# Seven block products in place of eight for the branch gates, and another order of the input projection, in a two-layer diffusion backbone

## What is computed

```python
h = rms_norm(x, p['norm1_w']) * (1 + sc1) + sh1
proj = h @ p['w_in']
hy, qkv, scv, gates = jnp.split(proj, [HY_COLS, HY_COLS + ATT_COLS, HY_COLS + ATT_COLS + SC_COLS], axis=-1)
...
ya = hyena_mixer(hy, ...)
q, k, v = jnp.split(qkv, [ATT_Q, ATT_Q + ATT_KV], axis=-1)
...
ga, gb, gc = jnp.split(gates, 3, axis=-1)
merged = (jax.nn.sigmoid(ga) * (ya @ p['w_br_a'])
          + jax.nn.sigmoid(gb) * (yb @ p['w_br_b'])
          + jax.nn.sigmoid(gc) * (yc @ p['w_br_c']))
```

## Time and profile before

| | us |
|---|---|
| median of 3 runs | 2319.89 (2317.75 to 2322.31) |
| the profiled execution (span from its first instruction to its last) | 2318.0 |
| TensorE busy in it (matmuls) | 2186.4 |
| VectorE, ScalarE, GpSimd busy | 1435.7, 1006.0, 184.3 |
| mean granted TensorE clock | 0.972 of full speed |

### The profile page before, as it was taken

One profiled execution on the slowest core, in us unless ns is written; L12 is line 12 of the kernel. 1 busy time (PEld: TensorE's weight loads), 2 busy tenths in 40 slices (PEclk: granted clock), 3 DMA queues, 4 the chain that ended last, 5 costly groups with the idle time before them and its releaser, 6 DMA issues.

```text
span 2318.0 us, 35033 instructions
## 1 busy us (share of the span) xinstructions
PE 2186.4 (94%) x13382; PEld 1763.0 (76%) x13382; DVE 1435.7 (62%) x2009; ACT 1006.0 (43%) x1486; POOL 184.3 (8%) x224
## 2 busy tenths in 40 slices
PE   7998999999988998799997999999998999699999
PEld 2447999999656997466666999999864899366665
DVE  4865532612677555899996443431368763699997
ACT  2433212223622124688884321222461222588885
POOL 0010000010100100121110000001100110011210
PEclk8999999999998999899998999999999999799999
DMA  9772222333313522999993122132413342699997
GB/s 355 262 265 97 73 73 74 112 122 113 140 48 125 174 86 91 383 388 379 387 393 112 57 81 80 70 135 104 159 59 126 134 144 73 243 386 386 387 378 273
DMA packets 72954, 436.14 MB, mean 188 GB/s; under 512 B 9289, under 2 KB 9929, under 8 KB 31930
## 3 DMA queue, kind: packets, MB, share of 16 engines
q1 hardware_dynamic: 46368, 331.89, 37.4%
q0 software_dynamic: 22160, 88.61, 11.8%
q10 hardware_dynamic: 4300, 13.90, 1.8%
HBM read 384.87 MB, written 49.50 MB: 187 GB/s over the span
## 4 chain that ended last, share of the span: by engine, by line
PE 77%; DVE 9%; ACT 4%; DMA 3%; issue 3%; DVEq 2%; ACTq 0%; POOL 0%; POOLq 0%
PE ps L637 39%; PE ps L1119 9%; PE ps L1145 5%; PE ps L1123 4%; PE ps L839 4%; PE ps L1149 2%; PE ps L736 2%; PE ps L718 2%; PE ps L896 2%; DVE back L1933 1%; PE ps L676 1%; DMA front<-kspec 1%; DVE nb L1902 1%; ACT front_r L1213 1%; ACT front L1406 1%
## 5 line engine op out<-in xcount | busy, mean ns | idle before, releaser
L637 PE MATMUL ps<-front_r 128*128 128x320 f32 x5696 | 899.6, 311 | 14.2 <-DVE back_r L1993 8.2
L637 PEld LDWEIGHTS ps<-front_r 128*128 128x128 f32 x5696 | 854.0, 189 | 16.6 <-DVE front_r L1604 8.9
L1604 DVE TENSOR_TENSOR front_r<-ring,front_r 128x1024 fp32r<-128x1024 f32 x148 | 181.1, 1224 | 467.6 <-ACT front_r L1213 466.5
L1213 ACT ACTIVATE front_r<-ring 128x1024 fp32r<-128x1024 f32 x180 | 190.0, 1056 | 376.8 <-PE ps L637 291.7
L1213 ACT ACTIVATE back<-ps 128x256 f32<-128x256 f32 (+4 forms) x176 | 88.5, 518 | 376.7 <-PE ps L637 152.6
L2087 DVE TENSOR_TENSOR back_r<-front,back_r 128x1024 fp32r<-128x1024 f32 x128 | 153.3, 1219 | 4.9 <-ACT back_r L1213 3.2
L1119 PE MATMUL ps<-back_r 128*80 128x512 f32 x384 | 152.1, 396 | 3.7 <-ACT back_r L1213 3.7
L1119 PE MATMUL ps<-back_r,front_r 128*80 128x512 f32 x384 | 151.9, 396 | 0.0
L637 PE MATMUL ps<-back_r,front_r 128*128 128x320 f32 x640 | 148.1, 313 | 0.0
L1213 ACT ACTIVATE back_r<-front 128x1024 fp32r<-128x1024 f32 x128 | 133.4, 1054 | 7.7 <-PE ps L1149 4.9
L1372 ACT ACTIVATE back<-ps 128x640 f32<-128x640 f32 x48 | 33.8, 704 | 227.2 <-PE ps L637 227.1
(11 more groups left out here) (250 smaller groups left out, 3200.6 us busy)
## 6 DMA issues: line engine op xcount, KB each, us to landing
ring<-in_stream SPq DMA_DIRECT2D x186, 1024.0 KB, 7.3
front<-in_stream SPq DMA_DIRECT2D x80, 1024.0 KB, 18.2
back<-in_stream SPq DMA_DIRECT2D x48, 1024.0 KB, 19.2
gates<-back POOLq DMA_DIRECT2D x48, 320.0 KB, 2.4
back<-gates POOLq DMA_DIRECT2D x48, 320.0 KB, 3.3
kspec<-back POOLq DMA_DIRECT2D x20, 512.0 KB, 7.1
front<-kspec POOLq DMA_DIRECT2D x4, 2048.0 KB, 11.0
rows<-front ACTq DMA_DIRECT2D x10, 520.0 KB, 3.9
```

The lines of the kernel that those rows point to most:

```text
L637: mm = pe.matmul(tokh(b)[:, c0:c1], w(wp)[:, k, :], src(hp, k)[:, c0:c1], start=first, stop=last)
L1213: return act.activation(o, i, ACT.Copy)
L1604: dve.tensor_tensor(half_dst(u, 1), src, half_dst(u, 0).bitcast(F32), ALU.subtract).then_inc(w_lo, 1)
```

## The change

A gate item keeps its 256 columns, but is laid out as four blocks of 512 inputs x 128 columns (weights A11, A12, A21, A22), and the tokens as four blocks too (inputs 0 to 511 or 512 to 1023, tokens 0 to 319 or 320 to 639). The four output blocks are made of seven block products in place of eight (Strassen's scheme in Winograd's form). A product (`product`) is 4 x 3 = 12 matmuls of 320 columns, so a group of seven is 84 where two chunks were 96. Two products are accumulated on others in PSUM; the other sums are made elsewhere:

- Four sums of weight blocks for each group, by GpSimd (`pool.tensor_tensor` on 128 x 512), into `wsum`.
- Four sums of token blocks for each layer, by VectorE (`token_sum`), split into parts by ScalarE (`sum_hi`) and VectorE (`sum_lo`).
- Seven operands of 128 x 512 for each group in place of two halves of 128 x 1024: high part on ScalarE (`operand_hi`), low part on VectorE (`operand_lo`), in four places `WG`.
- Five additions of a product in PSUM to a partial result in SBUF for each group, on VectorE (`gate_sum`); a copy and two sigmoids on ScalarE (`gate_taken`).

The layer's order becomes: queries, keys and values (now tile by tile behind the norm, `first_qkv`), gates, hyena, short convolution. The transposes of queries and keys stand behind chunks 9 to 14 of the hyena and short convolution, the prompt's scores behind chunk 16. The preparation of queries and keys on VectorE is cut into 19 pieces (`prepare`), behind products 0 and 2 of each group. The stores of gates move from GpSimd's queue to SyncE's, one of 640 KB behind the load of an item. The prompt's filter spectrum (`Kp`) is loaded behind the attention's end, with a semaphore of its own.

```diff
-P_HY = 0
+P_QKV = 0
+P_GATE = P_QKV + N_QKV
+P_HY = P_GATE + N_GATE
 P_SC = P_HY + N_HY
-P_QKV = P_SC + N_SC
-P_GATE = P_QKV + N_QKV
-P_BR = P_GATE + N_GATE
+P_BR = P_SC + N_SC
 P_WO = P_BR + N_BR
...
+        WG = region_r(40, [4, 2, 512])
+        T_hi, T_lo, T_x = region_r(56, [4, 4, TH]), region_r(76, [4, 4, TH]), region(76, [4, 4, TH])
+        sgb, wsum = region(121, [2, 4, TH]), region(131, [4, 512])
...
+        qT, kT = region(66, [4, T]), region(137, [P + PAST + LS])
...
+        SUMS = {1: 1, 3: 2, 4: 0, 6: 3}
+        BLOCKS = {0: 0, 2: 1, 5: 3}
+        def operand(l, n):
+            g, j = n // 7, n % 7
+            if j in SUMS:
+                return wsum[:, SUMS[j], :]
+            return home(place(l, P_GATE + g))[:, 512 * BLOCKS[j]:512 * BLOCKS[j] + 512]
+        def block_of(l, g, b):
+            return home(place(l, P_GATE + g))[:, 512 * b:512 * b + 512]
+        def wait_operand_place(eng, l, n):
+            wait_half_used(eng, l, U_GATE + n - 4 if n >= 4 else U_GATE - 2 + n // 2)
...
+                    i = g - place(l, P_GATE) - 4
+                    if 0 <= i < N_GATE:
+                        sp.wait_ge(sg_ready, l * N_GATE + i + 1)
+                        sp.dma_start(a["gates"][2 * i:2 * i + 2].rearrange("i p n -> p i n"),
+                                     sgb[:, i % 2].rearrange("p (i h) n -> p i (h n)", i=2)).then_inc(sg_stored[i % 2], 16)
...
+                pool.wait_ge(t_raw, 4 * (l + 1))
+                apart(pool)
+                for g in range(N_GATE):
+                    u = l * UNITS + U_GATE + 7 * g
+                    at = place(l, P_GATE + g)
+                    a11, a12, a21, a22 = (block_of(l, g, b) for b in range(4))
+                    pool.wait_ge(landed[slot_of(at)], landing(at))
+                    if g:
+                        pool.wait_ge(w_lo, u - 2)
+                    apart(pool)
+                    pool.tensor_tensor(wsum[:, 0, :], a21, a22, ALU.add).then_inc(w_sum, 1)
+                    pool.wait_ge(w_sum, l * 4 * N_GATE + 4 * g + 1)
+                    apart(pool)
+                    pool.tensor_tensor(wsum[:, 1, :], wsum[:, 0, :], a11, ALU.subtract).then_inc(w_sum, 1)
+                    pool.tensor_tensor(wsum[:, 2, :], a11, a21, ALU.subtract).then_inc(w_sum, 1)
+                    if g:
+                        pool.wait_ge(w_lo, u)
+                    pool.wait_ge(w_sum, l * 4 * N_GATE + 4 * g + 2)
+                    apart(pool)
+                    pool.tensor_tensor(wsum[:, 3, :], a12, wsum[:, 1, :], ALU.subtract).then_inc(w_sum, 1)
...
+                def first_qkv():
+                    for k in range(KC):
+                        if k % 4 == 0:
+                            half_ready(l, k // 4)
+                        pe.wait_ge(x_lo, l * OP + k + 1)
+                        for t in range(NT):
+                            for wp, hp in ((0, 0), (0, 1), (1, 0)):
+                                mm = pe.matmul(ps[:, t + 2 * (t // 4), 0:256], h_part(hp, k)[:, P * t:P * t + P],
+                                               w2(k // 4, 4, wp)[:, k % 4, :], start=k + wp + hp == 0,
+                                               stop=k == KC - 1 and wp == 1)
+                            if k == 3 and t == NT - 1 or k == KC - 1 and t in (1, 3, 4):
+                                mm.then_inc(qkv_ready, 1)
+                first_qkv()
+                for i in range(1, N_QKV):
+                    qkv_item(i)
...
+                def tokens_of(j, part):
+                    if j in (0, 2, 6):
+                        r0, c0 = ((0, 0), None, (4, 0), None, None, None, (4, TH))[j]
+                        return lambda k: (h_hi, h_lo)[part][:, r0 + k, c0:c0 + TH]
+                    t = {4: 0, 1: 1, 3: 2, 5: 3}[j]
+                    return lambda k: (T_hi, T_lo)[part][:, t, k, :]
+                def product(n):
+                    g, j = n // 7, n % 7
+                    bank = (0, 1, 0, 2, 4, 3, 4)[j]
+                    pe.wait_ge(w_lo, l * UNITS + U_GATE + n + 1)
+                    if j == 6:
+                        pe.sem_inc(item_used, 1)
+                    if g == 0 and j in (0, 1, 3, 5):
+                        pe.wait_ge(qkv_freed, 9 * l + (7 if j < 2 else 8))
+                    if g and j in (0, 1, 3, 5):
+                        pe.wait_ge(gate_act, (l * N_GATE + g) * 3 - 1)
+                        pe.wait_ge(gate_dve, (l * N_GATE + g) * 5 - (3 if j else 4))
+                    if j == 2:
+                        pe.wait_ge(gate_act, (l * N_GATE + g) * 3 + 1)
+                    if g and j in (3, 4, 5):
+                        pe.wait_ge(gate_dve, (l * N_GATE + g) * 5)
+                    if j == 6:
+                        pe.wait_ge(gate_dve, (l * N_GATE + g) * 5 + 3)
+                    hi, lo = tokens_of(j, 0), tokens_of(j, 1)
+                    w = WG[:, n % 4].rearrange("p a (k m) -> p a k m", k=4)
+                    for k in range(4):
+                        for wp, x in ((0, hi), (0, lo), (1, hi)):
+                            mm = pe.matmul(ps[:, bank, 0:TH], w[:, wp, k, :], x(k),
+                                           start=k == 0 and wp == 0 and x is hi and j not in (2, 6),
+                                           stop=k == 3 and wp == 1, skip_group_check=j in (2, 6))
+                    mm.then_inc(gate_made, 1)
+                pe.wait_ge(x_lo, l * OP + OP_Y)
+                for n in range(PRODUCTS):
+                    product(n)
...
+                for c in range(24):
+                    half_ready(l, U_HY + c)
+                    if c == 0:
+                        pe.wait_ge(gate_act, (l + 1) * 3 * N_GATE - 1)
+                        pe.wait_ge(gate_dve, (l + 1) * 5 * N_GATE - 4)
+                    elif c < 3:
+                        pe.wait_ge(gate_dve, (l + 1) * 5 * N_GATE - 2 + c)
+                    else:
+                        wait_chunk_freed(pe, l, c - 3)
+                    chunk(c % 3, lambda part: w2(c, KC, part), h_part, KC).then_inc(chunk_ready, 1)
+                    if 1 <= c <= 8:
+                        transposes(c - 1)
+                    if c == 9:
+                        pe.wait_ge(tr_evac, l * 8 + 8)
+                        pe.wait_ge(prep_done, l + 1)
+                        apart(pe)
+                    if 9 <= c <= 9 + NT:
+                        turn_qk(c - 9)
+                    if c == 16:
+                        prompt_scores()
...
+                        wait_chunk_freed(pe, l, 21)
+                        wait_chunk_freed(pe, l, 22)
+                        wait_chunk_freed(pe, l, 23)
...
+                def operand_hi(n):
+                    g, j = n // 7, n % 7
+                    wait_operand_place(act, l, n)
+                    if j in SUMS:
+                        act.wait_ge(w_sum, (l * N_GATE + g) * 4 + SUMS[j] + 1)
+                    elif j == 0:
+                        at = place(l, P_GATE + g)
+                        act.wait_ge(landed[slot_of(at)], landing(at))
+                    copy(WG[:, n % 4, 0, :], operand(l, n)).then_inc(w_hi, 1)
+                def gate_taken(n):
+                    g, j = n // 7, n % 7
+                    out, G = sgb[:, g % 2], l * N_GATE + g
+                    if j == 0:
+                        act.wait_ge(gate_made, l * PRODUCTS + n + 1)
+                        if G >= 2:
+                            act.wait_ge(sg_stored[g % 2], 16 * (G // 2))
+                        copy(out[:, 0, :], ps[:, 0, 0:TH]).then_inc(gate_act, 1)
+                    elif j == 2:
+                        act.wait_ge(gate_made, l * PRODUCTS + n + 1)
+                        act.wait_ge(gate_dve, 5 * G + 1)
+                        act.activation(out[:, 0, :], ps[:, 0, 0:TH], ACT.Sigmoid).then_inc(gate_act, 1)
+                    elif j == 6:
+                        act.wait_ge(gate_dve, 5 * G + 5)
+                        act.activation(out[:, 1:4, :], out[:, 1:4, :], ACT.Sigmoid).then_inc(gate_act, 1)
+                        act.drain().then_inc(sg_ready, 1)
...
+                for n in range(4):
+                    operand_hi(n)
+                for n in range(PRODUCTS):
+                    gate_taken(n)
+                    if n + 4 < PRODUCTS:
+                        operand_hi(n + 4)
+                    if n == 17:
+                        act.wait_ge(qs_ready, l + 1)
+                        act.activation(st5[:], st5[:], ACT.Sqrt, bias=eps[:, 0:1], scale=1.0 / HD).then_inc(qrt, 1)
+                    if n >= PRODUCTS - 2:
+                        split_after(l, U_HY + n - PRODUCTS + 2, U_HY - 3 + 2 * (n - PRODUCTS + 2))
...
+                def operand_lo(n):
+                    dve.wait_ge(w_hi, l * UNITS + U_GATE + n + 1)
+                    dve.tensor_tensor(WG[:, n % 4, 1, :], operand(l, n), WG[:, n % 4, 0, :].bitcast(F32),
+                                      ALU.subtract).then_inc(w_lo, 1)
+                def gate_sum(n):
+                    g, j = n // 7, n % 7
```

(39 more changed lines are left out.)

407 lines of the change are left out of this document (193 added, 214 removed).

## The result

| | before | changed |
|---|---|---|
| median of the runs, us | 2318.82 | 2360.69 |
| lowest to highest, us | 2314.52 to 2322.31 | 2358.47 to 2366.5 |
| ratio to before | | 1.0191, interval 1.0171 to 1.021 |
| span of the profiled execution, us | 2318.0 | 2357.0 |

What follows compares the result with a forecast made beforehand. TensorE's work was taken as the bound; -21.2 - 3.95 + 0.4 + 0.8 + 5.6 = -18.3 us a layer, -36.7 for two, gave 2281.3 against the profiled 2318.0, so 2283 for the median, range 2270 to 2355.

Steps and rivals of the forecast that it cites:

- What bounds the kernel: Stage between norm and attention: TensorE's work is the bound, its neighbours have room, so fewer matmuls are time won.
- Term 1: Gate products: 144 fewer matmuls of 320 columns at 0.147 us, -21.2 us for a layer.
- Term 2: TensorE's waits around transposes, gates and hyena go, -3.95 us; a longer wait before the scores adds 0.4.
- Term 3: Layer's start, from norm to first gate product: waits for ScalarE and reordered work cost +0.8 us a layer.
- the edge that it named: Layer's start: VectorE ready at about +19.4, just in time for the third item of queries, keys and values.
- Term 5: GpSimd's four weight sums a group, about 1.2 us each, hidden under TensorE; cost to VectorE taken as nothing.
- Term 4: Rhythm of a gate group: product 6 waits up to 0.8 us for VectorE's sum 4, +5.6 us a layer.
- the rule of the lock: VectorE with two SBUF inputs and a GpSimd instruction reading SBUF exclude each other for a whole instruction.
- The rival: Gate groups: GpSimd's sums shut out VectorE's two-input instructions for their whole length; about 2351 us, chance 0.32.

Runs made afterwards that it cites:

- e4: The changed kernel with VectorE's preparation pieces left out, only their signals kept (output not the reference's): 2280.23 us.
- e10: e6 with ScalarE's first copies ahead of the first token sum, the 960-element sigmoid later, and GpSimd's sums starting only after the token operands: 2274.96 us.
- e7: The changed kernel with the weight sums made by VectorE and the preparation pieces spread, one a group behind product 0: 2311.14 us.
- e1: The changed kernel with GpSimd's weight sums replaced by signals, except in layer 0's first group (output not the reference's): 2294.54 us.
- e8: e7 with ScalarE's first copies of queries, keys and values put ahead of the first token sum: 2306.78 us.
- e9: e8 with ScalarE's 960-element sigmoid moved behind the next group's first copy and rounding: 2275.16 us.
- e6: The changed kernel, sums still on GpSimd, with preparation pieces spread: one a group behind sum 5, two in groups 9 and 10, four in the hyena part: 2325.12 us.
- e5: The changed kernel with the weight sums made by VectorE in place of GpSimd, pieces where they were: 2327.8 us.

## Why the prediction was wrong, step by step

**What bounds the kernel.** Right that TensorE does. "Its neighbours have room" held for their sum, not for VectorE's stretch from product 0 to sum 4.

**Term 1** was right: in e4 the gates of layer 0 have one wait of 0.58 us, and start to end they take 148.9 us; 148.2 were worked out.

**Term 2.** The waits named are gone, but one of 1.63 us came, before the transposes of the keys (ScalarE has to empty the bank first), and the one before the scores is 1.07, 0.3 above before where 0.4 was counted:

```profile
539.32 0.77 PE L923 MATMUL ps<-ident,back 128*128 128x128 f32 x5 [1.63 <-ACT back L1501]
605.80 1.35 PE L969 MATMUL ps<-back 64*128 64x512 f32 x8 [1.07 <-DVE back L2080]
```

**Term 3** was right in its mechanism up to the edge that it named: from the norm's last low part at 193.63 (0 as before) the second item started at +5.6, as worked out. The third was to find VectorE ready at +19.4; it started at +24.2, behind 3.94 us of wait, because the four low parts of 1280 elements took up to 2.6 us each and not 1.42, beside GpSimd's first four sums. That is Term 5's error again. (Alone such a low part takes 1.48 us in e10, so 1.42 was a little short by itself.) The two starts lost 6.9 and 4.1 us, part of it at a lower clock (the third item of layer 0 takes 17.35 us at a granted clock of 0.82; 14.4 were worked out). In e7, with the order of the start as predicted and without that collision, the first product of layer 0 stands 48.5 us behind the first matmul (184.97 to 233.44), just as worked out: 36.4, and the 12.1 from the first matmul to the norm's end.

**Term 4** was right without the holds: e1 has it as forecast, product 6 waiting for sum 4, 5.9 us in layer 0 against 5.5. It had ScalarE's sigmoid ahead of the next group's first operand ("finishes what product 6 of the last group left it"), but not that this closes a loop with VectorE, which keeps a wait in nearly every group when VectorE's own chain is shortened (e8 against e9 shows it; for e6 only e10 speaks, which has two other moves as well).

**Term 5** is the step that failed: "So GpSimd gives way and VectorE does not, as far as a DMA's few reads can tell ... I take nothing, by that row". The cost of GpSimd's sums to VectorE, put at nothing, is up to 1.0 us for each sum. GpSimd's duration was near (1.29 for 1.2). But the row was of an indirect DMA, which shows nothing of an instruction that streams two operands: beside the four sums of the group shown VectorE's instructions grew by 0.9, 0.5, 1.0 and 0.9 us. I had the rule of the lock before me as a rival, and gave a row about another kind of instruction more weight than it could bear.

The rival's 2351 was close to the 2360.69 measured, and in part by accident. It had 39.5 us of waits for a layer; there are 25.7, and the 14.1 of longer matmuls, nearly all of it the lower granted clock, it did not have; nor did it have the losses of the start. The holds are shorter than the whole sum because each sum slips in between two of VectorE's instructions, and what of it lies under an addition from PSUM costs nothing. (Its figure for a sum of 0.97 us, 2335, comes to about 2331 by the same working; nothing rests on it.) Put together for layer 0: -18.3 forecast, +6.9 start, +34.3 gates, +1.6 for the new wait in the hyena part and -0.1 before the scores is +24.4; measured from first matmul to scores is 424.24 in place of 399.93 us, +24.3.

## What to carry to other kernels

Before work goes to GpSimd beside a busy VectorE, count VectorE's instructions with two operands in SBUF: each of GpSimd's that reads SBUF can cost VectorE most of its own length, here up to 1.0 of 1.29 us beside the operands, against the 0.7 that VectorE would need for the work itself. It is free only where VectorE has that much room before the next thing that TensorE waits for, so lay out the work between one such point and the next, not the sum over a group. When matmuls fall away, the neighbours' order has to be written anew: the same seven products cost 1.9% or give 1.8% by where eighteen small pieces, one sigmoid and the first copies stand, with GpSimd's first sums moved behind the token operands or its sums made by VectorE.

## What was not expected of the hardware

A wait of TensorE can cost more than itself. In the changed kernel and e5 the 24 matmuls behind a wait of up to 2.6 us took 3.78 us more often than not, behind a longer one mostly 5.0 to 6.5, and the granted clock of the changed kernel's gates was 0.93; without waits it was 0.99 to 1.00. Where the 24 took 6.52 us (from 330.51) the granted clock is 0.52, near the lower of its two levels, 1.2 GHz; where they took 3.78 (from 348.63) it is 1.00, the upper one, 2.4 GHz. It isn't the length of the wait alone: waits of 1.76 us were followed by 5.31 in e8 and by 3.78 in e7, in e5 one of 2.59 by 3.78 and one of 2.11 by 5.31, and in its second layer one of 3.46 by 3.78. What decides whether the clock falls stays open; here some 12 us a layer hung on it.

GpSimd's durations by operands read from SBUF, 128x512 in fp32: none (fill) 0.53 us, one (copy) 0.61, two (sum) 1.29, the last two each as the shortest record. In the record an instruction that is held looks like a longer one, not like idle time, on either engine; the shortest of a group beside its longest shows it.
